# Attention in groups of two pairs, norms on GpSimd, half of the copies on VectorE

## The chip, the cores and the metric

The kernel runs on one core of a Trainium2 chip. The metric is the device time of one execution in microseconds. TensorE multiplies, VectorE (DVE) and ScalarE (ACT) work on its results in PSUM (8 banks) and on data in SBUF, GpSimd (POOL) on data in SBUF only, and SyncE starts the loads of the weights.

## What is computed

Two transformer blocks of two layers each on 512 tokens of width 1024, in fp32. The first block mixes NSA attention, a linear recurrence (RG-LRU) and a convolution with a layer norm. The second has attention layers (full A and windowed B with a sink in layer 0; latent C and neighbourhood D in layer 1), a cross attention X to a memory of 256 tokens, and a SwiGLU feed-forward. Cut to what the change touches, each attention is

```python
s = einsum('qd,kd->qk', q, k) * scale        # NSA, A, B, D: 64 wide; C: 64 + 32 (rope) wide
p = softmax(where(mask, s, NEG))             # NSA: times a gate per query and branch
o = einsum('qk,kd->qd', p, v)
```

with 8 heads of 64 and query blocks of 128. NSA has three branches (compressed keys, selected, window), whose gated outputs are added. The layer norm of the convolution is

```python
mu = mean(u); var = mean(square(u - mu))
un = (u - mu) * rsqrt(var + EPS) * ln_g + ln_b
```

## The kernel before, in words

The program is a list of stages (`PROGRAM`). Most of the span are matrix products: "strips" of 128 output columns, whose weights are loaded in pieces, split by ScalarE (high part, line 1226) and GpSimd (low part, line 2212, `w_lo`), and multiplied three times (lines 861 to 863). Between them stand seven attention stages: NSA twice, AB2, D2, C2, X2 twice.

An attention stage is a list of tiles: one head, 128 queries, up to 512 keys. Tiles come in pairs of two heads that use the two halves of TensorE's rows. NSA has 72 tiles (36 pairs), AB2 64, D2 and C2 32 each, X2 8. A tile goes through these steps, and every engine has its own program for them, which it runs in order:

- TensorE: `scores` (three products, lines 1067, 1070 and 1076; for compressed keys 1059) into one of 3 or 4 score banks.
- VectorE: `maxed` (lines 1933, 1935) scales, masks and takes the maximum; ScalarE: `exps` (1421) with the row sum.
- VectorE: `normed`: the reciprocal of a pair's two sums (1961), and two multiplications of a tile by its reciprocal, in NSA also by the gate (1965, 1967).
- TensorE: `turn` transposes the tile (1090) into bank 4 or 5; ScalarE: `copy` brings it back to SBUF (1432, ring `PT` of 4).
- TensorE: `values` (1100, 1103) into bank 6 or 7; VectorE: `output` (1977, 1979).

TensorE's order per pair s is: scores of pair s, turns of pair s - 2 (`TURN_LAG`), values of pair s - 3 (`VALUE_LAG`). VectorE and ScalarE go tile by tile. `extras(part)` hangs other work at numbered moments (one per tile): in NSA the layer norm of the convolution (sums and spreads over bank 0, `ln_sum`, `ln_spread`, `ln_var`, `ln_factor`, `ln_spread_factor`, lines 1153, 1159, 2012 to 2024; its squares on GpSimd in `layer_norm`, 2183 to 2193), high and low parts of the mixed output (`split`), and in D2 the load and scaling of biases. `DRAIN` gives the chunks of the next strip that TensorE does in the last steps of a stage, and `warm` (line 868) issues dummy products, in NSA in front of tile 30 too.

GpSimd runs through all pieces of weights in one loop; its layer norm and `rope_keys` stand at fixed pieces in it.

## Time and profile before

| | us |
|---|---|
| median of 3 runs | 2272.75 (2271.89 to 2274.1) |
| span of the profiled execution | 2275.0 |
| TensorE busy in it | 2199.9 (97%) |
| VectorE busy | 1246.9 (55%) |
| ScalarE busy | 1078.0 (47%) |
| GpSimd busy | 853.7 (38%) |

The profile is of one execution. Its own time is known as its span of 2275.0 us, from first to last instruction; it lies 2.25 us above the median. Busy time of TensorE is counted from modelled ends of pipelined products, so 97% doesn't mean full rate: what one instruction costs is the distance of its start to the next one's.

In the table by stage below (rows 2) the columns are: the stretch, its length in us, busy us (and instructions) of PE, PEld, DVE, ACT and POOL, the granted clock of TensorE as a share of 2.4 GHz, the DMA share and GB/s. A row of a timeline is: start and length in us, engine, line, operation, operands, how many, and in brackets the idle time before it and what ended it. The page's line of the chain (rows 1) gives shares of the span.

### The profile page before, as it was taken

The numbers are of one execution on the slowest core, as the hardware profiler recorded it, in microseconds if no ns is written. First come the engines' busy times: TensorE is split into PE (matmuls) and PEld (weight loads), VectorE is DVE, ScalarE is ACT, GpSimd is POOL, SyncE is SP. The second block draws the span as 40 slices with busy tenths as digits, with TensorE's granted clock in tenths as the row PEclk, the third lists the DMA queues.
The fourth block names the chain that finished last, engine by engine and source line by source line (L and its number), as shares of the span: only waits on it lengthen the run. The fifth ranks groups of instructions, "written<-read, shape, count | busy, mean of one in ns | idle before, by whom it ended". The sixth has DMA issues, their size and how long they took to land.

```text
span 2275.0 us, 33281 instructions
## 1 busy us (share of the span) xinstructions
PE 2199.9 (97%) x12130; PEld 1763.7 (78%) x12130; DVE 1246.9 (55%) x2614; ACT 1078.0 (47%) x2160; POOL 853.7 (38%) x665
## 2 busy tenths in 40 slices
PE   8999899999999999989999999999999999999997
PEld 6778667888866788668888888888767888888886
DVE  6997782499778446885552112234666655211222
ACT  6542484465247652685453223343566545322332
POOL 4333304443330343104255545554110425554553
PEclk9999899999999999999999999999999999999998
DMA  5334002332410233203233333343110323333331
GB/s 171 85 91 141 25 2 79 104 91 79 144 38 11 75 89 109 68 2 110 67 94 96 95 109 98 92 124 95 48 60 20 111 66 97 94 95 100 98 96 66
DMA packets 107186, 189.74 MB, mean 83 GB/s; under 512 B 12049, under 2 KB 22801, under 8 KB 106897
## 3 DMA queue, kind: packets, MB, share of 16 engines
q1 hardware_dynamic: 101136, 178.67, 27.3%
q10 hardware_dynamic: 5888, 8.95, 1.2%
q8 instruction: 99, 1.62, 0.3%
q14 instruction: 63, 0.51, 0.1%
HBM read 182.85 MB, written 2.10 MB: 81 GB/s over the span
## 4 chain that ended last, share of the span: by engine, by line
PE 85%; DVE 10%; issue 3%; ACT 2%; POOL 1%; DMA 0%; SPq 0%; DVEq 0%; ACTq 0%
PE bank L861 23%; PE bank L863 23%; PE bank L862 23%; PE bank L1090 3%; PE bank L1103 3%; PE bank L1076 2%; DVE temp L1933 1%; DVE bank L2053 1%; PE bank L868 1%; DVE temp L1965 1%; PE bank L1067 1%; PE bank L1070 1%; PE bank L931 1%; DVE temp L1967 1%; POOL w_lo L2212 1%
## 5 line engine op out<-in xcount | busy, mean ns | idle before, releaser
L2212 POOL TENSOR_TENSOR w_lo<-w_raw,w_hi 128x512 fp32r<-128x512 f32 (+3 forms) x618 | 824.7, 1341 | 1337.1 <-ACT w_hi L1226 1336.7
L861 PE MATMUL bank<-op_hi,w_hi 128*128 128x512 f32 x1840 | 734.4, 399 | 9.1 <-POOL w_lo L2212 4.4
L863 PE MATMUL bank<-op_hi,w_lo 128*128 128x512 f32 x1840 | 719.4, 391 | 0.0
L862 PE MATMUL bank<-op_lo,w_hi 128*128 128x512 f32 x1840 | 719.4, 391 | 0.0
L1226 ACT ACTIVATE w_hi<-w_raw 128x512 fp32r<-128x512 f32 (+2 forms) x634 | 385.4, 617 | 682.5 <-PE bank L863 678.8
L861 PEld LDWEIGHTS bank<-op_hi,w_hi 128*128 128x128 f32 x1840 | 347.1, 189 | 95.7 <-issue 15.3
L862 PEld LDWEIGHTS bank<-op_lo,w_hi 128*128 128x128 f32 x1840 | 347.6, 189 | 73.4 <-issue 4.1
L863 PEld LDWEIGHTS bank<-op_hi,w_lo 128*128 128x128 f32 x1840 | 347.1, 189 | 73.7
L1648 DVE TENSOR_TENSOR temp<-bank,rstd 128x512 f32<-128x512 f32 x151 | 104.4, 691 | 396.0 <-PE bank L863 378.2
L861 PE MATMUL bank<-side_hi,w_hi 128*128 128x512 f32 (+1 forms) x628 | 233.2, 371 | 2.5 <-DVE side_lo L1730 1.4
L863 PE MATMUL bank<-side_hi,w_lo 128*128 128x512 f32 (+1 forms) x628 | 230.9, 368 | 0.0
L862 PE MATMUL bank<-side_lo,w_hi 128*128 128x512 f32 (+1 forms) x628 | 230.8, 367 | 0.0
L1718 DVE TENSOR_TENSOR x_t<-bank,x_t 128x512 f32<-128x512 f32 x80 | 55.3, 691 | 314.3 <-PE bank L863 314.1
L1421 ACT ACTIVATE temp<-temp,small 128x512 f32<-128x512 f32 (+3 forms) x288 | 174.0, 604 | 14.0 <-DVE small L1933 6.7
L1432 ACT ACTIVATE temp<-bank 128x512 f32<-128x512 f32 (+3 forms) x304 | 140.8, 467 | 83.0 <-PE bank L1090 81.6
L2053 DVE SCALAR_TENSOR_TENSOR bank<-conv_area,par,bank 128x512 f32<-128x512 f32 x232 | 174.9, 754 | 6.8
L1090 PE MATMUL bank<-consts,temp 128*128 128x128 f32 x864 | 132.7, 283 | 34.2 <-DVE temp L1967 12.5
L1090 PEld LDWEIGHTS bank<-consts,temp 128*128 128x128 f32 x864 | 93.4, 141 | 81.6 <-issue 35.0
L861 PEld LDWEIGHTS bank<-side_hi,w_hi 128*128 128x128 f32 x628 | 118.4, 188 | 25.1 <-DVE side_lo L1730 2.7
L863 PEld LDWEIGHTS bank<-side_hi,w_lo 128*128 128x128 f32 x628 | 118.4, 188 | 19.6
L862 PEld LDWEIGHTS bank<-side_lo,w_hi 128*128 128x128 f32 x628 | 118.4, 189 | 19.4 <-issue 0.5
L1103 PE MATMUL bank<-temp,vz 128*64 128x128 f32 x1312 | 100.4, 290 | 0.0
(269 smaller groups left out, 2256.3 us busy)
## 6 DMA issues: line engine op xcount, KB each, us to landing
w_raw<-in_weights SPq DMA_DIRECT2D x620, 256.0 KB, 2.7
w_raw<-in_weights SPq DMA_DIRECT2D x32, 192.0 KB, 2.3
temp<-temp SPq DMA_DIRECT2D x40, 64.0 KB, 2.0
x_t<-in_x SPq DMA_DIRECT2D x8, 256.0 KB, 5.4
conv_area<-in_mem ACTq DMA_DIRECT2D x2, 1024.0 KB, 5.5
out_y<-ybuf SPq DMA_DIRECT2D x8, 256.0 KB, 2.1
conv_area<-in_bias ACTq DMA_DIRECT2D x1, 1920.0 KB, 8.0
conv_area<-in_bias ACTq DMA_DIRECT2D x2, 960.0 KB, 4.9
```

The costliest lines, as they stand in the source:

```text
L861: pe.matmul(dst, w[0], m[0], start=start, stop=False)
L862: pe.matmul(dst, w[0], m[1], start=False, stop=False)
L863: return pe.matmul(dst, w[1], m[0], start=False, stop=stop)
L1090: ins = pe.transpose(bank[4 + a % 2][:, P * b:P * b + P], E[a % E_RING][:, P * b:P * b + P], ident)
L1103: ins = pe.matmul(dst, t["pv"][b], PT[a % PT_RING][:, P * b:P * b + P], start=t["start"] and b == 0, stop=t["stop"] and last)
L1226: act.activation(w_hi[:, j, 0:m * w], w_raw[:, p % RAW_RING, 0:m * w], ACT.Copy).then_inc(*mark("weights_high", p))
L1421: act.activation(e, e, ACT.Exp, bias=m, scale=-1.0, accum_out=total).then_inc(*mark("exps", a))
L1432: act.activation(PT[a % PT_RING][:, 0:n], bank[4 + a % 2][:, 0:n], ACT.Copy).then_inc(*mark("probs_copied", a))
L1648: return dve.tensor_tensor(dst, strip_bank(n)[0:rows, 0:s.cols], f[0:rows, 0:s.cols], ALU.mult)
L1718: dve.tensor_tensor(x_t[:, s.idx, :], src[:, :], x_t[:, s.idx, :], ALU.add).then_inc(*mark("strip_taken", n))
L2053: settle(dve.scalar_tensor_tensor(out=acc[:, c, :] if j == CONV_K - 1 else run, in0=u_conv[:, c, j:j + T], scalar=w, in1=run, op0=ALU.mult ...
L2212: pool.tensor_tensor(w_lo[:, j, 0:n], w_raw[:, p % RAW_RING, 0:n], w_hi[:, j, 0:n].bitcast(F32), ALU.subtract).then_inc(*mark("weights_spl ...
```

## The change

Tiles of NSA, AB2, D2 and C2 are now worked on in groups of two pairs (`PAIRS`); X2 stays at one. TensorE's order per group s is: scores of both pairs of group s, values of group s - 2, turns of group s - 1. In C2 a group takes its two pairs from neighbouring head chunks, so that the four 32-wide rope parts lie in the four quarters of the rows; their products are issued for all four tiles behind both 64-wide parts. The norm multiplications of all tiles but NSA's compressed ones move from VectorE to GpSimd. Tiles 1 and 3 of a group are copied by VectorE instead of ScalarE. Groups write their outputs four tiles at a time (NSA: 18 as before, but with one output bank, 6). Score tiles use 4 banks throughout, turned tiles banks 4, 5 and a third; layer norm sums move to bank 7. The rings grow (`E_RING` 6 to 8), extras move to the end of a group's step, GpSimd's loop over pieces is cut by stages, with the layer norm spread over its steps.

```diff
-TURN_LAG = 2
-VALUE_LAG = 3
+PAIRS = {"NSA": 2, "AB2": 2, "D2": 2, "C2": 2, "X2": 1}
+TURN_LAG = {1: 2, 2: 1}
+VALUE_LAG = {1: 3, 2: 2}
+NEXT_SPLIT = 10
+VECTOR_COPIES = (1, 3)
-E_RING = 6
+E_RING = 8
-SCORES = (1, 2, 3)
+SCORES = (1, 2, 3, 0)
-WARM_TURN = {"NSA": {30: 3}, "AB2": {0: 1}, ...
+WARM_TURN = {"NSA": {}, "AB2": {0: 2}, ...
...
+                    t["out"], t["out_held"] = (6, at_group - 1) if step[1][0] == "NSA" else (6 + at_group % 2, at_group - 2)
+                    t["turn"] = 4 + n % 2
+                    if PAIRS[step[1][0]] == 2:
+                        third = t["out"] if step[1][0] != "NSA" else 7 if n >= LN_TILES else 4
+                        t["turn"] = (4, 5, third, 4 if third != 4 else 5)[n % 4]
...
+                def latent_scores(group):
...
+                    for pair in group:
+                        free_banks(pair)
+                        for x, y in parts:
+                            for t in pair:
+                                pe.matmul(score_bank(t), t["q"][x], t["k"][y], start=(x + y == 0), stop=False)
+                    for x, y in parts:
+                        for t in group[0] + group[1]:
+                            ins = pe.matmul(score_bank(t), t["more"][0][x], t["more"][1][y], start=False, stop=(x == 1))
...
+                    if PAIRS[part[0]] == 2:
+                        for pair in in_group(groups, s - value_lag):
+                            values(pair)
+                    for pair in in_group(groups, s - turn_lag):
+                        for t in pair:
+                            turn(t)
...
+                    if scaled_by_pool(part, t):
+                        dve.reciprocal(total, total).then_inc(*mark("sums_inverted", a))
+                        return
...
+                        for pair in before[:1]:
+                            normed(pair)
+                        for t in to_max[:2]:
+                            maxed(t)
+                        for pair in before[1:]:
+                            normed(pair)
+                        for t in to_max[2:3]:
+                            maxed(t)
+                        for t in [pair[1] for pair in in_group(groups, s - value_lag)]:
+                            if t["last"]:
+                                output(t)
+                        for t in to_copy[:1]:
+                            copy(t)
+                        for t in to_max[3:]:
+                            maxed(t)
+                        for t in to_copy[1:]:
+                            copy(t)
...
+            def attend(part):
+                groups, l = groups_of(part), part[1]
+                def scaled(pair):
+                    t = pair[0]
+                    pool.wait_ge(*after("sums_inverted", pair[1]["a"]))
+                    total, _ = pair_sums(t)
+                    for r, t in enumerate(pair):
+                        e = E[t["a"] % E_RING][:, 0:t["nk"]]
+                        if t["gate"] is not None:
+                            ins = pool.tensor_scalar(e, e, total[:, r:r + 1], t["gate"], ALU.mult, ALU.mult)
+                        else:
+                            ins = pool.tensor_scalar(e, e, total[:, r:r + 1], C("ones")[:, 0:1], ALU.mult, ALU.mult)
+                        ins.then_inc(*mark("probs_scaled", t["a"]))
+                if part[0] == "NSA":
+                    norm_added(l)
+                for s in range(steps_of(part)):
+                    if part[0] == "NSA" and s == 7:
+                        norm_squares(l, 0, 2)
+                    for pair in in_group(groups, s - 1):
+                        if scaled_by_pool(part, pair[0]):
+                            scaled(pair)
+                    if NEXT_SPLIT in moments_of(part, s):
+                        split_to(last_of(FOLLOWS[part] + 1))
...
```

## Rows read from the trace of the kernel before

**Rows 1.** The page: share of the span of each engine on the chain.

```profile
PE 85%; DVE 10%; issue 3%; ACT 2%; POOL 1%; DMA 0%; SPq 0%; DVEq 0%; ACTq 0%
```

**Rows 2.** Busy time by stage: NSA, AB2, D2, C2; columns below.

```profile
241.70:352.50 110.80, 100.44 (x903) 72.51 (x903) 85.48 (x294) 78.55 (x227) 13.76 (x12) 0.92 0.03 6
...
927.80:1024.80 97.00, 87.88 (x844) 63.95 (x844) 82.89 (x311) 82.25 (x236) 5.36 (x4) 1.00 0.08 23
1617.60:1673.00 55.40, 51.75 (x495) 37.64 (x495) 43.76 (x131) 43.05 (x102) 2.59 (x4) 1.00 0.13 40
1694.40:1763.70 69.30, 69.30 (x606) 48.16 (x606) 45.14 (x134) 45.64 (x107) 5.38 (x4) 1.00 0.11 32
```

**Rows 3.** Timeline of TensorE, one pair of AB2: start, length, line, count.

```profile
951.95 0.50 PE L1076 MATMUL bank<-side_hi 64*128 64x512 f32 x2
...
952.86 1.09 PE L1090 MATMUL bank<-consts,temp 128*128 128x128 f32 x8
953.88 1.09 PE L1103 MATMUL bank<-temp,vz 128*64 128x128 f32 x16
954.91 0.50 PE L1076 MATMUL bank<-side_hi 64*128 64x512 f32 x2
```

**Rows 4.** Timeline of TensorE, AB2's windowed tiles, four pairs.

```profile
998.67 0.45 PE L1076 MATMUL bank<-side_hi 64*128 64x384 f32 x2
...
1009.26 0.44 PE L1076 MATMUL bank<-side_hi 64*128 64x384 f32 x2
...
1010.98 0.67 PE L1090 MATMUL bank<-consts,temp 128*128 128x128 f32 x4 [0.92 <-DVE temp L1967]
```

**Rows 5.** Timeline of TensorE, start of AB2, two pairs of scores.

```profile
928.39 0.39 PE L1076 MATMUL bank<-side_hi,side_lo 64*128 64x512 f32 x2
928.62 0.40 PE L1076 MATMUL bank<-side_hi 64*128 64x512 f32 x2
```

**Rows 6.** Short stretches of transposes and values; line 1090 (min/median/max ns).

```profile
950.40 0.60 PE L1090 MATMUL bank<-consts,temp 128*128 128x128 f32 x4
...
951.42 0.61 PE L1103 MATMUL bank<-temp,vz 128*64 128x128 f32 x8
...
L1090 PE MATMUL bank<-consts,temp x864: 270/273/473, 251.8 to 1873.3; 128*128 128x128 f32 x173
```

**Rows 7.** Timeline of TensorE, one pair of C2.

```profile
1714.14 0.50 PE L1067 MATMUL bank<-op_hi 64*128 64x512 f32 x2
...
1715.04 0.50 PE L1070 MATMUL bank<-side_hi 32*128 32x512 f32 x2
...
1715.93 1.11 PE L1090 MATMUL bank<-consts,temp 128*128 128x128 f32 x8
...
1717.99 0.50 PE L1067 MATMUL bank<-op_hi 64*128 64x512 f32 x2
```

**Rows 8.** Instructions by form, VectorE, AB2: count | busy us, mean ns.

```profile
L1935 DVE TENSOR_SCALAR_CACHE_REDUCE temp<-bank 128x512 f32<-128x512 f32 x32 | 21.5, 685 | 4.8 <-PE bank L1076 4.8
L1967 DVE TENSOR_SCALAR temp<-temp,small 128x512 f32<-128x512 f32 x32 | 16.0, 541 | 0.6
...
L1961 DVE RECIPROCAL small<-small 128x2 f32<-128x2 f32 x32 | 5.2, 163 | 0.6
```

**Rows 9.** Instructions by form, GpSimd, whole span.

```profile
L2212 POOL TENSOR_TENSOR w_lo<-w_raw,w_hi 128x512 fp32r<-128x512 f32 x572 | 783.8, 1377 | 1219.1 <-ACT w_hi L1226 1218.6
...
L2190 POOL TENSOR_TENSOR conv_area<-conv_area 128x512 f32<-128x512 f32 x8 | 8.3, 1040 | 42.9 <-DVE conv_area L2012 42.9
...
L2202 POOL CAST side_hi<-temp 128x512 fp32r<-128x512 f32 x1 | 0.6, 612 | 0.0
```

**Rows 10.** Timeline of VectorE while GpSimd splits weights.

```profile
945.71 1.53 DVE L1967 TENSOR_SCALAR temp<-temp,small 128x512 f32<-128x512 f32 x2
```

**Rows 11.** Timeline of TensorE, NSA, in front of the second spread.

```profile
291.93 2.84 PE L868 MATMUL bank<-consts 128*128 128x512 f32 x6
295.25 1.00 PE L1090 MATMUL bank<-consts,temp 128*128 128x128 f32 x6 [0.48 <-DVE temp L1965]
```

More of the change, by code:

```diff
@@ L278, in build @@
         sp8 = sb("sp8", [P, 8])
[L279 removed]
+        small = sb("small", [P, 256])
         PAD = CONV_K - 1
@@ L600, in build @@
                     t["a"], t["g"] = at_tile, at_group
-                    banks = SCORES if step[1][0] == "NSA" and at_tile - ts[0]["a"] < LN_TILES else SCORES + (0,)
-                    t["bank"] = banks[(at_tile - ts[0]["a"]) % len(banks)]
+                    n = at_tile - ts[0]["a"]
+                    t["bank"] = SCORES[n % len(SCORES)]
                     t["held"] = held.get(t["bank"])
@@ L765, in score_bank, with grouped, by_vector, copied @@
             return bank[t["bank"]][:, 0:t["nk"]]
+        def grouped(part):
+            return PAIRS[part[0]] == 2
+        def by_vector(part, t):
+            return grouped(part) and (t["a"] - ATT[part][0]["a"]) % 4 in VECTOR_COPIES
+        def copied(part, a):
+            t = ATT[part][a - ATT[part][0]["a"]]
+            return after("probs_copied_vector" if by_vector(part, t) else "probs_copied", a)
+        def scaled_by_pool(part, t):
+            return grouped(part) and not t["cmp"]
         def tables_of(s):
@@ L1039, in attend, with free_banks, scores @@
                 steps = DRAIN[part[0]]
-                def scores(pair):
-                    for t in pair:
+                def free_banks(tiles_of):
+                    for t in tiles_of:
                         if t["held"] is not None:
                             pe.wait_ge(*after("maxed", t["held"]))
-                        if part[0] == "NSA" and t["a"] == ts[LN_TILES]["a"]:
-                            pe.wait_ge(*after("ln_scaled", (part[1], 3)))
-                    if part[0] == "C2" and pair is pairs[0]:
+                def latent_scores(group):
+                    parts = ((0, 0), (0, 1), (1, 0))
+                    if group[0][0]["a"] == ts[0]["a"]:
                         pe.wait_ge(*after("rope_keys", 0))
+                    for pair in group:
[6 more added lines that the diff above has]
+                            ins = pe.matmul(score_bank(t), t["more"][0][x], t["more"][1][y], start=False, stop=(x == 1))
+                            if x == 1:
+                                ins.then_inc(*mark("scores", t["a"]))
+                def scores(pair):
+                    free_banks(pair)
                     if pair[0]["cmp"]:
@@ L1108, in values @@
                     for t in pair:
-                        pe.wait_ge(*after("probs_copied", t["a"]))
-                        if t["first"] and t["g"] >= 2:
-                            pe.wait_ge(*after("outputs_taken", t["g"] - 2))
+                        pe.wait_ge(*copied(part, t["a"]))
+                        if t["first"] and t["out_held"] >= 0:
+                            pe.wait_ge(*after("outputs_taken", t["out_held"]))
+                        if t["first"] and t["size"] == 4:
+                            pe.wait_ge(*copied(part, t["a"] + 2))
                     blocks = range(len(pair[0]["pv"]))
@@ L1984, in attend @@
+                for s in range(steps_of(part)):
+                    if NEXT_SPLIT in moments_of(part, s):
                         split_to(last_of(FOLLOWS[part] + 1))
-                    if i < len(ts):
-                        maxed(ts[i])
-                    if NORM_LAG <= i < len(ts) + NORM_LAG and i % 2 == 1:
-                        normed(ts[i - NORM_LAG:i - NORM_LAG + 2])
-                    if OUT_LAG <= i < len(ts) + OUT_LAG and ts[i - OUT_LAG]["last"]:
-                        output(ts[i - OUT_LAG])
@@ L1991, in attend @@
[L1991 to L1996 removed]
+                    now, before = in_group(groups, s), in_group(groups, s - 1)
+                    if PAIRS[part[0]] == 1:
+                        for t in [t for pair in now for t in pair][:1]:
+                            maxed(t)
+                        for t in [pair[1] for pair in in_group(groups, s - value_lag - 1)]:
+                            if t["last"]:
+                                output(t)
+                        for t in [t for pair in now for t in pair][1:]:
+                            maxed(t)
+                        for pair in before:
+                            normed(pair)
+                    else:
+                        to_max = [t for pair in now for t in pair]
+                        to_copy = [t for pair in before for t in pair if by_vector(part, t)]
+                        for pair in before[:1]:
[3 more added lines that the diff above has]
+                        for pair in before[1:]:
+                            normed(pair)
+                        for t in to_max[2:3]:
+                            maxed(t)
+                        for t in [pair[1] for pair in in_group(groups, s - value_lag)]:
+                            if t["last"]:
+                                output(t)
+                        for t in to_copy[:1]:
+                            copy(t)
+                        for t in to_max[3:]:
+                            maxed(t)
+                        for t in to_copy[1:]:
+                            copy(t)
@@ L1998, in extra_stage @@
+                    for i in moments_of(part, s):
+                        for stage in between.get(i - LOW_LAG[PAIRS[part[0]]], ()):
+                            if stage[0] in LATE_LOWS:
+                                extra_stage(*stage)
+                        for stage in between.get(i, ()):
+                            if stage[0] not in LATE_LOWS:
+                                extra_stage(*stage)
             def extra_stage(kind, l, c=None):
```

275 lines of the change are left out of this document (158 added, 117 removed).

## The prediction

> **What bounds the kernel now.** I read the chain of work that ended last first: TensorE carries 85% of it, GpSimd 1% [rows 1]. So what counts is TensorE's own work plus its waits. The change touches only the attention stages. The second view is the table of busy time by stage [rows 2]: the two NSA stages (one row is shown, 110.8 us; the other lasts 112.6 us and looks the same), AB2 97.0, D2 55.4 and C2 69.3 us, 445 us in all. The reader is to see three things there. TensorE is idle for 10.4, 9.1, 3.6 and 0.0 us in the four kinds. VectorE and ScalarE are at 71 to 85% in NSA and AB2, GpSimd at 5 to 12% everywhere. And the granted clock is 0.92 in NSA and 1.00 elsewhere.
>
> The third view is TensorE's timeline in the first half of AB2 (full rows of 512 keys) [rows 3]. One pair takes 2.96 us (951.95 to 954.91) with no idle: scores 0.91, eight transposes 1.02, sixteen value instructions 1.03. So here TensorE is the bound, and no relief of the other engines helps by itself. The second half of AB2 differs: four pairs take 10.59 us (998.67 to 1009.26), 2.65 each, and TensorE stands 0.92 us for VectorE's scaled tile [rows 4]. There VectorE is the bound.
>
> **What the regrouping takes off TensorE.** Inside a pair TensorE changes three times between ways of using its array: half-height (scores), full (transposes), half-width (values). What a change costs is read by comparing with runs without one. At the start of AB2 two pairs of scores stand directly behind each other: the last pass of one begins at 928.39, the first pass of the next at 928.62, 0.23 us [rows 5]. Three such passes are 0.69 us; the pair above takes 0.91. Four transposes without a change among them last 0.60, of which the last one's own length is 0.273 (the median of that line): 0.11 us each, 0.87 for eight, against 1.02 [rows 6]. Value instructions run two by two: eight last 0.61, 0.11 us per two, 0.87 for sixteen, against 1.03 [rows 6]. Sum without changes 2.43, with them 2.96: I take 0.50 us per pair for all three. The changed kernel does scores of two pairs, values of two, turns of two: the same three changes per two pairs. That saves 0.25 us a pair wherever TensorE is the bound.
>
> **C2 gains more.** Its scores have a part of 64 rows (1714.14 to 1715.04, 0.90 us) and a part of 32 rows (to 1715.93, 0.89 us), and one pair takes 3.85 us [rows 7]. The change does both 64-row parts, then one 32-row part in which the four tiles of a group sit in four different quarters of the array. Per group, before: 2 x 1.79 = 3.58. After: 0.91 + 3 x 0.23 = 1.60, plus 0.89 if four small products run side by side as two do now: 2.49. Saved 1.09, plus 0.30 from the two other kinds of change: 1.39 per group, 8 groups, 11.1 us. Bounds for the four side by side: 0.69 us more per group (5.5 us in all) if they run two by two, nothing if all four overlap. I take nothing, since two of 32 rows take as long as two of 64 [rows 7]: the rows in use don't set the time. The Trainium skill ("TensorE: Matmul & The Clock Gate", section Measured speedup vs the span model) gives 3.07 times, not 4, for four tiles of 32 rows; by it, as an estimate, the block would be a third longer and C2 would gain 1.7 us less. No row here shows four at once.
>
> **What GpSimd gets, and whether it is covered.** VectorE's two norm multiplications (541 ns each [rows 8]) leave it, and two copies of turned tiles per group come to it from ScalarE. The same copy from PSUM has no row on VectorE; a 512-wide op from PSUM takes 685 ns there [rows 8]. Per group of full tiles VectorE then has 4 x 0.69 of maxima, 2 x 0.16 of reciprocals, 2 x 0.69 of copies and one output: under 4.9 us against 5.9 now on TensorE. It isn't the bound. GpSimd's multiplication of a 128x512 tile by two scalars has no row. From below: its one-input cast of that size takes 612 ns. From above: its two-input subtraction takes 1377 ns [rows 9]. The new op reads one tensor as the cast does, so I take 0.7 us, and keep 0.61 to 1.38. The Trainium skill ("GPSIMD Engine Reference", Elementwise side-by-side cycle accounting) names 769 ns for a well unrolled loop over 512 elements; at that price the sum below doesn't change. Its section Engine selection says to keep elementwise work off this engine, which speaks against this change and is rival 3.
>
> The four multiplications of a group are serial, and their place in the chain decides. VectorE's order is: ..., copy of tile 1, maximum of tile 3, copy of tile 3, then the first reciprocal of that next group. The copy of tile 3 waits for TensorE's last transposes of the step. So the loop is: transposes of tile 3 (0.60), copy (0.69), reciprocal (0.16 [rows 8]), four multiplications, transposes of tile 3 again, with some 0.2 us of hand-offs (estimate): 1.65 + 4p. Where p is 0.7 that is 4.5 us, hidden behind TensorE's 2 x 2.71 = 5.4. With the copy of tile 1 and the last maximum in front of it the chain allows p up to about 0.87; from p = 1.06 the loop is longer than the 5.9 us of today. GpSimd does no harm to VectorE's reads of PSUM: the maxima take 685 ns on average. It does to VectorE's doubled-rate multiplications: two of them took 1.53 us at 945.7 [rows 10], while GpSimd was splitting weights, against a mean of 541 ns for one [rows 8]. These leave VectorE, so this stops.
>
> **The sum by stage**, against the profiled execution of 2275.0 us:
> AB2, full tiles: 16 pairs x 0.25 = 4.0 us.
> AB2, windowed tiles: VectorE loses two multiplications a pair and gets one copy; TensorE's floor falls too. I take 0.25 a pair here as well, 4.0 us. Bounds 0 (the in-order waits for turned tiles eat it) and 10 (TensorE's floor).
> D2: 16 x 0.25 = 4.0, and 0.5 from VectorE's freed time beside the bias scaling: 4.5.
> C2: 11.1.
> NSA, each: 36 x 0.25 = 9.0. Against it: the single output bank, where values of a new head pair wait within a step for VectorE's output (twice, about 1.4 each: 2.8); the square root of the layer norm, whose spread now stands in the same step as its factor. TensorE bridges this with 2.84 us of dummy products (removed by the change) and stands 0.48 more [rows 11], 3.3 us; after the change ScalarE comes to the root only behind its last exponential of the step, and I expect a bare wait of 4.5, 1.2 more. At the end all four silu stages come in one step and the first value of the next strip comes later: 1.2. Fewer waits for VectorE and ScalarE in the narrow tiles: +1.2 back (bounds 0 and 7, the larger part of the idle time). Net 5.0 each, 10.0 for both.
> Weight splits: in AB2 and C2 four pieces are now queued on GpSimd in front of a group's multiplications, 4 x 1.377 = 5.5 us [rows 9]. The slack of that step covers about 3 of it: 2.5 and 2.0 lost. In NSA the seven layer norm ops (1040 ns and more [rows 9]) stand between multiplications too, but tiles are narrow there: covered, and 8 us on the path per stage if p is high.
> Sum: 4.0 + 4.0 + 4.5 + 11.1 + 10.0 - 4.5 = 29.1 us. The profiled execution would take 2245.9 us; it lies 2.25 us above the median of 2272.75, so the median goes to 2243.6. I say 2244.
>
> **Rivals.**
> 1. The forecast, 2244: p below 0.9, changes of array use halved. Speaks for it: rows 3 to 7 price the changes directly. Chance 0.55.
> 2. NSA also gets its clock back and loses its idle time. A mean clock of 0.92 over 110.8 us is 8.9 us per stage, 17 in all: 2272.75 - 29 - 17 = 2227. For: fewer idle gaps. Against: the table-load wait stays. Chance 0.12.
> 3. GpSimd is the bound, at p = 1.3. Loop 1.65 + 5.2 = 6.85 against 5.9: +0.95 in 16 groups of AB2 and D2, +15. C2 about -2 (its step is 7.7 now). NSA: +0.5 in 18 groups and 6 for the layer norm, +15 each, +30. Weight splits uncovered in AB2, D2 and C2: +2. Total +45: 2318. It decides from p = 1.06. For: all its two-input ops of this size take 1.04 to 1.38. Against: the cast at 612 ns. Chance 0.17.
> 4. The change doesn't do what it says: the PE waits take the place of the array changes, because turned tiles, copies and maxima stand in one order on VectorE, and p is near 1. Then only C2's packing (9) and a few us remain: 2262. It speaks for it that the lag from scores to turns is now one step, and the sum of all waits in one step counts. Chance 0.16.
>
> **How the numbers follow.** Two times within 0.2% (4.5 us) can't be told apart for this kernel. Faster: rivals 1 and 2 whole and most of 4, 0.55 + 0.12 + 0.10 = 0.77. Same: 0.05, the slow end of rival 4. Slower: 0.17 + 0.01 = 0.18. Range 2218 to 2290: it takes in the unknown C2 packing, both ends of AB2's windowed half, rival 4, rival 2 and the mild part of rival 3 (p to 1.15), and leaves out the rest of 3 and what lies beyond 2.
>
> **What the profile after would show.** In AB2's first half a group period of 5.4 us with scores x4, values x32, transposes x16 and no idle in front of the transposes: right; 6 or more with transposes waiting for GpSimd: rival 3. GpSimd's 128x512 row by two scalars: 0.6 to 0.9 right, over 1.06 wrong. In C2 a 32-row block of 0.9 us for four tiles and a group of 6.3 us; a block of 1.6 would take 5.5 us away. In NSA idle time in front of the first value of a new head pair and one of about 4.5 us in front of the second spread; a clock of 1.0 there speaks for rival 2. Outside the attention stages nothing should move by more than 1 us; if it does, the ordering of weight splits on GpSimd is what I missed.

## The result

The changed kernel takes 2294.8 us (median, 2287.46 to 2296.41), against 2273.43 for the kernel before in the same comparison. The ratio is 1.0077, 95% interval 1.0057 to 1.0096: slower by 0.77%, 17.5 us (the two medians lie 21.4 apart). The forecast was 2244, range 2218 to 2290, so the time lies outside the range, on the wrong side: the time was to fall and it rose. Timed again beside the kernel before, the changed one gives 1.0073 (1.0054 to 1.0092).

Where the time went is read best as distances from the start of one attention stage to the start of the next (the first score product of each). These rows are the table of busy time for the changed kernel, from NSA 1 to NSA 2, NSA 2 to AB2, AB2 to the first X2, D2 to C2, and C2 to the second X2. Columns are those of rows 2.

```profile
241.80:666.60 424.80, 398.45 (x2246) 321.35 (x2246) 281.60 (x567) 199.66 (x385) 178.81 (x173) 0.95 0.25 73
666.60:956.00 289.40, 265.42 (x1690) 212.19 (x1690) 165.69 (x418) 132.88 (x302) 119.91 (x126) 0.93 0.22 62
956.00:1139.80 183.80, 175.12 (x1337) 141.56 (x1337) 121.68 (x346) 114.02 (x286) 88.91 (x96) 1.00 0.22 64
1642.30:1717.80 75.50, 67.49 (x567) 49.75 (x566) 53.75 (x132) 46.07 (x111) 34.67 (x48) 1.00 0.19 59
1717.80:1872.00 154.20, 150.07 (x1098) 122.31 (x1097) 87.07 (x194) 82.32 (x173) 70.21 (x64) 0.99 0.27 76
```

The same distances in the kernel before, its second NSA stage as a row, the others in the table behind it:

```profile
650.80:927.80 277.00, 263.97 (x1696) 204.72 (x1696) 176.25 (x446) 143.99 (x338) 82.27 (x62) 0.97 0.23 65
```

| from | before | after | measured | forecast |
|---|---|---|---|---|
| NSA 1 | 409.1 | 424.8 | +15.7 | -5.0 |
| NSA 2 | 277.0 | 289.4 | +12.4 | -5.0 |
| AB2 | 187.3 | 183.8 | -3.5 | -5.5 |
| D2 | 76.9 | 75.5 | -1.4 | -4.5 |
| C2 | 159.6 | 154.2 | -5.4 | -9.1 |
| sum | | | +17.8 | -29.1 |

The spans differ by 2292.9 - 2275.0 = 17.9 us, so nothing else moved. AB2, D2 and C2 went the forecast way, by 10.3 instead of 19.1 us. The two NSA stages turned the sign. The NSA windows themselves answer to the first line of rows 2:

```profile
241.80:368.30 126.50, 103.89 (x897) 81.45 (x897) 75.09 (x266) 67.46 (x191) 51.84 (x76) 0.82 0.02 6
666.60:791.50 124.90, 102.33 (x897) 80.08 (x897) 75.04 (x266) 67.44 (x191) 51.77 (x76) 0.84 0.02 6
```

TensorE is idle for 22.6 us instead of 10.4, and its granted clock is 0.82 instead of 0.92. VectorE and ScalarE have less to do than before (75 and 67 us against 85 and 79), so no engine became the bound. The second view is TensorE's list of waits, longest sums first:

```profile
PE bank L911 <- DVE op_lo L1667: 12.1, 2, 6.0
PE bank L1228 <- DVE small L2151: 8.2, 2, 4.1
PE bank L1149 <- POOL temp L2343: 7.9, 6, 2.2
```

Two of them, once per NSA stage each, are new: 6.0 us in front of the next strip (it needs the silus), and 4.1 us in front of the second spread. In rows 11 the place of the second had 2.84 us of dummy products and 0.48 us of wait. What the clock did behind the 4.1 us is seen in a narrow window of each kernel, ten microseconds from where TensorE goes on; the changed kernel stands first, then the kernel before at the same place of its program:

```profile
299.50:309.50 10.00, 10.00 (x73) 9.00 (x71) 2.21 (x8) 1.44 (x2) 2.71 (x4) 0.50 0.01 2
```

```profile
295.00:305.00 10.00, 9.17 (x106) 7.65 (x106) 8.05 (x28) 5.97 (x17) 0.00 (x0) 1.00 0.01 2
```

0.50 is the 1.2 GHz level. TensorE is busy for all of those 10.00 us and gets 73 instructions started; the kernel before starts 106 in 9.17 busy us at 2.4 GHz. (The mix of products is not quite the same, so the counts show the direction and not the exact price.)

A third stretch of half clock comes earlier in the stage, in the changed kernel:

```profile
275.50:289.10 13.60, 12.10 (x76) 8.93 (x76) 5.94 (x27) 5.61 (x20) 7.38 (x11) 0.50 0.01 2
```

No wait of TensorE around its start is longer than 1.47 us. In the second NSA stage it lasts as long (from 698.8); the kernel before has 6.8 us of half clock at this place in its first stage and 3.4 in its second.

In the distance of NSA 2 the parts can be told apart. Idle time went from 277.00 - 263.97 = 13.0 to 289.40 - 265.42 = 24.0 us: +11.0. A granted clock of c over t us costs (1 - c) x t while TensorE is busy: 0.03 x 277.0 = 8.3 before, 0.07 x 289.4 = 20.3 after, +12.0 (each to about 1.4, since the clock is given in hundredths). Together +23, of which +12.4 were seen. So TensorE's own work at full clock became some 10.5 us shorter; 2.84 of it are the dummy products, and the rest fits the array changes, which no run tested in NSA by themselves. The forecast for the same three terms was +6.8 of idle time (2.8 + 4.0 + 1.2 - 1.2), nothing for the clock, and -11.8 of work (9.0 and the 2.84 of dummy products). So the forecast of the work was near; idle time was 4 us short, and the clock was missing.

### The profile page after: what moved, and what is told of

Same layout as the page of the kernel before. It is cut to its first block, busy times and chain, and to the rows that moved or that the text cites. A ratio compares the mean times of both kernels' runs of the same rounds, so it can differ in the third digit from the quotient of the medians.

```text
span 2292.9 us, 33268 instructions
## 1 busy us (share of the span) xinstructions
PE 2192.0 (96%) x12120; PEld 1780.0 (78%) x12120; DVE 1205.9 (53%) x2462; ACT 1027.1 (45%) x2024; POOL 1021.7 (45%) x921
## 3 DMA queue, kind: packets, MB, share of 16 engines
q8 instruction: 99, 1.62, 0.3%
## 4 chain that ended last, share of the span: by engine, by line
PE 86%; DVE 7%; issue 2%; ACT 2%; POOL 2%; DMA 0%; SPq 0%; DVEq 0%; ACTq 0%
PE bank L911 23%; PE bank L913 23%; PE bank L912 23%; PE bank L1149 4%; PE bank L1162 4%; PE bank L1129 3%; DVE bank L2183 1%; POOL w_lo L2384 1%; PE bank L918 1%; DVE temp L2024 1%; PE bank L981 1%; PE bank L1123 1%; PE bank L1030 1%; PE bank L1108 0%; POOL temp L2345 0%
## 5 line engine op out<-in xcount | busy, mean ns | idle before, releaser
L911 PE MATMUL bank<-op_hi,w_hi 128*128 128x512 f32 x1840 | 733.4, 399 | 20.3 <-DVE op_lo L1667 12.1
L2345 POOL TENSOR_SCALAR temp<-temp,small,consts 128x512 f32<-128x512 f32 (+2 forms) x128 | 92.2, 733 | 118.4 <-DVE small L2053 118.3
L2343 POOL TENSOR_SCALAR temp<-temp,small,gates 128x128 f32<-128x128 f32 (+3 forms) x128 | 76.8, 612 | 121.6 <-DVE small L2053 121.6
```

The source lines that it names most:

```text
L911: pe.matmul(dst, w[0], m[0], start=start, stop=False)
L2343: ins = pool.tensor_scalar(e, e, total[:, r:r + 1], t["gate"], ALU.mult, ALU.mult)
L2345: ins = pool.tensor_scalar(e, e, total[:, r:r + 1], C("ones")[:, 0:1], ALU.mult, ALU.mult)
```

## Experiments

Theory A: the NSA stages lose by two new waits and, more than that, by the half clock that follows a standstill (a time in which TensorE does nothing). Rivals: the waits alone are the loss (B), or GpSimd's multiplications are (C).

### Both waits removed

```diff
-DRAIN = {"NSA": ((), (0, 0), (), (0, 0, 1, 1, 1, 1)),
+DRAIN = {"NSA": ((), (), (), (0, 1, 0, 1, 0, 1, 0, 1)),
-    at(37 + c, "ln_scale", l, c)
-    at(72 + c // 2, "ln_silu", l, c)
-    at(74 + c // 2, "ln_split", l, c)
+    at(40 + c, "ln_scale", l, c)
+    at(72 + c, "ln_silu", l, c)
+    at(72 + c, "ln_split", l, c)
-at(72, "gate_silu", l)
+at(76, "gate_silu", l)
-at(35, "ln_spread_factor", l)
+at(38, "ln_spread_factor", l)
```

> Two edits of the changed kernel's NSA stage at once: the second spread of the layer norm stands one step later (moment 38, its scalings at 40 to 43), and at the end each silu is followed at once by its own high part, the gate's silu comes last, and TensorE does the last values before it starts the next strip. Theory A (bare waits in NSA cost their own time and pull the clock down): an NSA stage up to the next strip goes from 126.5 us to about 108, the whole from 2295 to 2258, below the kernel before (2273). Theory B (the clock falls because of the grouping of narrow tiles, whatever the waits): only the waits of 4.1 and 6.0 us go, 116 us per stage, the whole about 2275, granted clock in NSA stays near 0.82.

Measured: 2264.01 us, ratio to the kernel before 0.9958 (0.9937 to 0.9979). Table of busy time, the NSA windows of this kernel:

```profile
243.30:348.40 105.10, 90.02 (x890) 70.00 (x890) 72.42 (x262) 62.56 (x184) 51.73 (x76) 0.94 0.02 6
651.30:756.40 105.10, 89.74 (x890) 69.34 (x890) 72.28 (x262) 62.88 (x183) 51.84 (x76) 0.94 0.02 7
```

The two orders cost the changed kernel its loss: 27 us came back by the two ratios (31 by the medians), and the result is faster than both kernels. It lies between A's 2258 and B's 2275, nearer to A, and the clock in the windows is 0.94, not B's 0.82. GpSimd's busy time is as in the changed kernel (51.7 against 51.8), which speaks against C. The end of the stage was reordered, so the windows don't hold the same products (890 against 897); the distances do. The two NSA distances together fell from 714.2 to 682.3 us. Of these 31.9 us, 8.7 are idle time (50.3 to 41.6) and 23.2 busy time with the same work: the clock is the larger part.

### Each wait alone

The spread alone is the lines with `ln_scale` and `ln_spread_factor` of the diff above; the end alone is the rest of it.

> Only the second spread and its scalings moved one step later. Both theories: the wait of 4.11 us in front of it goes. Theory A: the 10.2 us at half clock behind it go too, 5 us more, NSA 126.5 to 117. Theory B: the clock falls all the same, NSA 122.5.

> Only the end of NSA: silu and high part in turn, gate silu last, last values before the next strip. Theory A: the wait of 6.03 us shrinks to 1 or 2, the half clock behind it (6.8 us) goes; last values and two rows of the next strip are done 7 us earlier, NSA 126.5 to about 119. Rival: the table load and the four silus set the time of the next strip in any order, gain under 3 us.

Measured, one execution each: 2273.19 and 2285.58 us. The two NSA distances sum to 694.0 us with the spread mended, 703.7 with the end mended and 682.3 with both. In the changed kernel they sum to 714.2, but to 706.5 in its second profile (the run further down), because there the first stage's stretch of half clock at 275 lasts 3.4 us instead of 13.7. So single executions can't price the waits closely: the spread is worth 12 to 20 us for the two stages, the end 3 to 12. The second NSA stage gives a like comparison for the spread, since that stretch lasts 13.7 us in both profiles of the changed kernel and in this one. Its distance with the spread mended:

```profile
653.40:936.10 282.70, 260.34 (x1692) 207.13 (x1692) 164.80 (x418) 132.98 (x302) 120.25 (x126) 0.95 0.22 63
```

Against 289.40 with 265.42 busy, 6.7 us are gone, 5.1 of them busy time and only 1.6 idle time, since other waits grew. So the wait of 4.1 us cost some 6.7 us here, and most of that was clock.

### The norms back on VectorE

```diff
 def scaled_by_pool(part, t):
-    return grouped(part) and not t["cmp"]
+    return False
```

(VectorE's `normed` multiplies by sum and gate instead.)

> The norm multiplications of the grouped stages go back to VectorE, all else as in the changed kernel. Theory A: GpSimd is not what costs in NSA, which stays within 3 us of 126.5; in AB2 VectorE has 6.0 us of work per group of full tiles against TensorE's 5.4, so AB2 gets 4 to 6 us longer than 92.8. Rival C (the hand-over to GpSimd is the loss, since TensorE waits 1.05 and 2.17 us for it in narrow groups): NSA gets 5 us or more shorter.

Measured: 2339.78 us, one execution. C falls: the distances of the two NSA stages grew by 10.8 and 13.7 us where C wanted them shorter, and within this grouping the multiplications on GpSimd are worth 45 us. The expectation was off too, since it had NSA within 3 us and AB2 4 to 6 longer; AB2's distance grew by 11.7. A full group of AB2 takes 5.94 us instead of 5.42, so VectorE doesn't carry them beside two copies per group. The granted clock of the whole execution is 0.968, against 0.977 in the changed kernel: more waits, less clock again.

### Dummy products in the waits

If the half clock behind a standstill is the loss, filling the wait with products that nobody needs should bring time back, though nothing that counts moves.

```diff
 elif kind in ("ln_spread", "ln_spread_factor"):
+    if kind == "ln_spread_factor":
+        pe.wait_ge(*after("ln_mean_square", l))
+        warm(7, 3)
     pe.wait_ge(*after("ln_mean" if kind == "ln_spread" else "ln_factor", l))
```

> The changed kernel with one addition: in front of the second spread of each NSA stage TensorE runs three dummy products of 512 columns (2.8 us, as the kernel before had them) as soon as VectorE has read the variance sums, inside the 4.1 us in which it stood still at 299.04. Nothing that anyone waits for moves: VectorE's factor is still ready at 298.98, so the spread starts at the same moment. Theory A (half of the loss in NSA is the granted clock, which falls behind such a standstill): the half-clock stretch at 299.5 (10.2 us) goes or shrinks to one of 3.4, and each NSA stage is 3 to 6 us shorter; the run comes out 6 to 12 us below the changed kernel, 2283 to 2289 us. Theory B (the waits alone cost the time, and the clock falls for its own reasons): no change, 2292 to 2297 us.

Measured: 2280.19 us, ratio 1.0012 (0.9997 to 1.0027). That is 14.6 us below the changed kernel's 2294.8 and 10.9 below the 2291.13 of its second timing; by the ratios some 14. A expected 6 to 12. Timeline of TensorE at the spread, and the ten microseconds behind it:

```profile
296.37 2.84 PE L918 MATMUL bank<-consts 128*128 128x512 f32 x6 [0.72 <-DVE small L2148]
299.76 1.16 PE L1231 MATMUL bank<-consts,small 128*128 128x128 f32 x8 [0.54 <-DVE small L2154]
```

```profile
299.80:309.80 10.00, 9.75 (x103) 8.57 (x105) 3.98 (x13) 3.33 (x7) 3.03 (x4) 0.83 0.01 2
```

The spread still starts where VectorE's factor lets it, 0.72 + 2.84 + 0.54 = 4.10 us behind the work in front. Behind it the clock is 0.83 instead of 0.50, and 103 instructions start instead of 73. B falls: the 4.1 us weren't shortened, only filled.

The counterpart is the kernel before without its dummy products:

```diff
-WARM_TURN = {"NSA": {30: 3}, "AB2": {0: 1}, "D2": {0: 2}, "C2": {0: 2}, "X2": {0: 2}}
+WARM_TURN = {"NSA": {}, "AB2": {0: 1}, "D2": {0: 2}, "C2": {0: 2}, "X2": {0: 2}}
```

> The kernel before, with one thing taken away: the three dummy products of 2.84 us that fill the wait at 291.93 in each NSA stage (those that the change also removes). No one waits for them, so by the waits alone nothing moves: TensorE stands still for 3.3 us and goes on at 295.25 as it does now. Theory A (the clock falls behind a standstill, and that is a large part of the loss): a half-clock stretch of some 7 to 10 us appears behind 295, each NSA stage is 3 to 5 us longer, the run 6 to 10 us above the kernel before. Theory B: no difference, within 2 us of the kernel before.

Measured: 2278.52 us, ratio 1.0013 (1.0003 to 1.0022): 3 us, between A's 6 to 10 and B's 2 at most, so by its time this run doesn't decide. Timeline at the wait, then the windows behind it:

```profile
295.85 1.51 PE L1090 MATMUL bank<-consts,temp 128*128 128x128 f32 x6 [3.33 <-DVE temp L1965]
```

```profile
295.90:299.10 3.20, 3.20 (x19) 2.54 (x20) 2.49 (x8) 2.33 (x7) 0.00 (x0) 0.50 0.02 5
299.30:309.30 10.00, 9.20 (x112) 7.61 (x110) 7.44 (x28) 4.66 (x15) 0.00 (x0) 1.00 0.00 1
```

The clock fell here too, but was back after 3.4 us, where the changed kernel stayed at half clock for 10.2. So a standstill of 3.33 us and one of 4.11 are not priced alike. In the changed kernel the 13.7 us of half clock had ended 5.7 us before the wait; between them TensorE was nearly always busy (0.3 us idle from 288.00 to the wait). Whether the length, what went before or what came behind makes the difference wasn't settled.

Two more runs put dummy products at the stage's end as well, and the first missed its place.

```diff
+if part[0] == "NSA":
+    warm(3, 11)
 drain(part, steps[3])
```

> The changed kernel once more, on the same chip as the next run, so that the two can be set side by side. If the fall of the granted clock in the NSA stages is a property of the kernel, 2290 to 2297 us again and some 40 us of half clock per NSA stage; if it is partly chance, single executions scatter between 2280 and 2297 with half-clock stretches between 27 and 48 us per stage.

> The changed kernel with dummy products in two of its waits in each NSA stage: three in front of the second spread (the run before with these alone gave 2280) and eleven of 512 columns (about 4.9 us) behind the last transposes, inside the 6.03 us in which TensorE waits at 362.25 for the silus. No product that counts is moved. Theory A (what follows a standstill is half clock, and that is most of the loss): the half-clock stretch of 6.8 us at 360.8 and its twin at 784.1 go, another 3 us each, 2272 to 2277, 18 to 22 us below the changed kernel of this call with all its waits still there. Theory B (the waits themselves are the loss): no difference between this run and the changed kernel beyond 3 us.

Measured: the changed kernel again 2291.13 (2287.05 to 2297.49); the one with dummy products 2298.79. The half clock is partly chance: in this profile of the same kernel the first NSA stage's distance is 417.3 us instead of 424.8, the second's 289.2 (289.4). The stretch behind the spread is in both stages 10.2 us long again, but in the first it began 2.5 us before the wait's end. The 6.03 us are in front of the second drain of strips, not the last, and eleven products are 22 instructions:

```profile
361.80 9.71 PE L918 MATMUL bank<-consts 128*128 128x512 f32 x22
```

The next product that counts starts at 370.94, so 9.1 us a stage are added work. Without them 2298.8 - 18.2 = 2280.6: 10.5 us below the changed kernel beside it, and in line with the run that has the spread's dummy products alone. The second form has six products where the wait is:

```diff
+if part[0] == "NSA" and s - len(groups) == 1:
+    warm(3, 6)
 if 0 <= s - len(groups) < 3:
     drain(part, steps[s - len(groups)])
```

> The changed kernel with three dummy products in front of the second spread of each NSA stage (as e5) and six (12 instructions, 5.3 us) directly behind the transposes that end at 356.2, in the 6.03 us in which TensorE waits for the silus. Nothing that counts is moved. Theory A (half clock follows a standstill): the half-clock stretch of 6.8 us behind it goes in both stages, 3 us each, the run 5 to 7 us below e5's 2280, 2273 to 2275. Theory B: no difference from e5, 2279 to 2281.

Measured: 2276.62 us, ratio 0.9999 (0.9988 to 1.001). The clock behind the wait, in the changed kernel (behind 6.03 us of standstill) and here (behind 0.89):

```profile
361.00:367.60 6.60, 5.35 (x30) 4.36 (x32) 2.50 (x4) 1.94 (x4) 0.00 (x0) 0.50 0.01 2
```

```profile
357.50:364.10 6.60, 5.84 (x48) 4.75 (x49) 3.96 (x7) 2.61 (x5) 0.28 (x1) 1.00 0.01 2
```

Here the stretch of half clock is gone, as A says. In the total it brings 3.6 us against the spread's dummies alone (A expected 5 to 7), and the two intervals overlap, so this share is shown in the windows and only likely in the time. With both, the changed kernel stands level with the kernel before: its whole loss, 0.77%, was bought back with products that compute nothing, which B can't explain. Removing the waits themselves brings another 0.4%.

### Array use, C2's packing, GpSimd's loop

The first puts scores, values and turns of AB2 and D2 back pair by pair inside a group.

```diff
+if part[0] in ("AB2", "D2"):
+    for k in range(2):
+        if k:
+            for pair in in_group(groups, s)[1:]:
+                scores(pair)
+        for pair in in_group(groups, s - value_lag)[k:k + 1]:
+            values(pair)
+        for pair in in_group(groups, s - turn_lag)[k:k + 1]:
+            for t in pair:
+                turn(t)
```

> The changed kernel, but within a group of AB2 and D2 scores, values and transposes are done pair by pair, so that TensorE changes its way of using the array six times per group instead of three. By the forecast a set of three changes costs 0.50 us: the period of a full group goes from 5.42 back to 5.9, AB2 about 4 us longer (8 full groups by 0.5) and D2 some 3. If the gain of the full groups did not come from these changes but from VectorE's freed time, the period stays at 5.42.

Measured: 2327.42 us, one execution. The period of a full group is 6.7, not 5.9; AB2's distance grew by 19.0 us and D2's by 11.8, where 4 and 3 were expected. Timeline of TensorE, score and transpose rows of one group:

```profile
977.95 0.50 PE L1129 MATMUL bank<-side_hi 64*128 64x512 f32 x2
...
979.87 1.09 PE L1149 MATMUL bank<-consts,temp 128*128 128x128 f32 x8
980.89 0.50 PE L1129 MATMUL bank<-side_hi 64*128 64x512 f32 x2
...
983.33 1.38 PE L1149 MATMUL bank<-consts,temp 128*128 128x128 f32 x8 [0.45 <-POOL temp L2355]
984.64 0.50 PE L1129 MATMUL bank<-side_hi 64*128 64x512 f32 x2
```

The half that doesn't wait lasts 980.89 - 977.95 = 2.94 us, as long as a pair of the kernel before (rows 3: 2.96). Two such halves are 5.88 against 5.42, the period in the changed kernel:

```profile
982.88 0.50 PE L1129 MATMUL bank<-side_hi 64*128 64x512 f32 x2
988.30 0.50 PE L1129 MATMUL bank<-side_hi 64*128 64x512 f32 x2
```

So three changes cost 0.46, and a pair saves 0.23 (forecast 0.25). The other half takes 3.75: TensorE stands 0.45 us for GpSimd's products in front of the transposes, which then take 1.31 instead of 1.02. The expectation hadn't that. It reads as if grouping didn't only save changes, but also gave the chain of maximum, exponential and multiplication the time to run; no run tests this by itself.

The second takes C2's 32-row parts pair by pair.

```diff
-for x, y in parts:
-    for t in group[0] + group[1]:
+for pair in group:
+    for x, y in parts:
+        for t in pair:
```

> The changed kernel, but C2's 32-row score parts are done for two tiles at a time instead of four. If four small products ran side by side as fast as two (the forecast), the part grows from 0.9 to 1.6 us: +0.69 us per group, C2's windows 5.5 us longer. If the hardware already ran them two by two, nothing changes. By a quarter lost of the fourfold overlap, +0.4 per group.

Measured: 2285.08 us, one execution; C2's distance 152.9 against 154.2, and its group still 6.33. Timeline of TensorE, the 32-row part, in the changed kernel and then in this one:

```profile
1746.04 0.51 PE L1111 MATMUL bank<-side_hi 32*128 32x512 f32 x4
1746.37 0.40 PE L1111 MATMUL bank<-side_lo,side_hi 32*128 32x512 f32 x4
1746.61 0.40 PE L1111 MATMUL bank<-side_hi,side_lo 32*128 32x512 f32 x4
```

```profile
1743.35 0.52 PE L1112 MATMUL bank<-side_hi 32*128 32x512 f32 x4
1743.69 0.42 PE L1112 MATMUL bank<-side_lo,side_hi 32*128 32x512 f32 x4
1743.92 0.42 PE L1112 MATMUL bank<-side_hi,side_lo 32*128 32x512 f32 x4
```

Twelve products of 32 rows take 0.9 us in either order; the second pair's first products start beside the first pair's, although four others stand ahead of them in the program. So the edit didn't make two by two out of four at once, and can't price that; what it shows is that four products on the four quarters take no longer than the two of rows 7 did, whatever the order. The forecast's 0.89 for the block holds. The Trainium skill ("TensorE: Matmul & The Clock Gate", Measured speedup vs the span model) gives 3.07 times for four tiles of 32 rows, by which the block would be longer; this trace doesn't show that, with 0.90 us for twelve.

The third doubles GpSimd's price of a tile.

```diff
+if part[0] in ("AB2", "D2"):
+    ins.then_inc(*mark("pool_step"))
+    pool.wait_ge(*after("pool_step"))
+    ins = pool.tensor_scalar(e, e, C("ones")[:, 0:1], C("ones")[:, 0:1], ALU.mult, ALU.mult)
 ins.then_inc(*mark("probs_scaled", t["a"]))
```

> The changed kernel, but GpSimd multiplies each tile of AB2 and D2 a second time, by ones: p goes from 0.77 to 1.6 us. By the loop that I wrote down (1.65 + 4p, TensorE's floor 5.42) the period of a full group becomes 8.0 us: +2.6 in each of some 7 full groups of AB2 and 8 of D2, narrow groups +1.5: D2 +18, AB2 +30. If GpSimd's product is hidden with much more slack than the loop says (the loop is wrong), the period stays near 5.4 to 6.5.

Measured: 2363.84 us, one execution. Timeline of GpSimd, the first multiplication of two groups:

```profile
988.64 0.77 POOL L2345 TENSOR_SCALAR temp<-temp,small,consts 128x512 f32<-128x512 f32 x1 [2.13 <-DVE small L2053]
...
990.26 0.77 POOL L2345 TENSOR_SCALAR temp<-temp,small,consts 128x512 f32<-128x512 f32 x1
...
996.82 0.77 POOL L2345 TENSOR_SCALAR temp<-temp,small,consts 128x512 f32<-128x512 f32 x1 [1.67 <-DVE small L2053]
```

A tile now costs 990.26 - 988.64 = 1.62 us, the period is 996.82 - 988.64 = 8.18. The loop that the prediction wrote down gives 1.65 + 4 x 1.62 = 8.13. AB2's distance rose by 43 us (183.8 to 227.1), D2's by 26.5, more than the expected 30 and 18: their clocks fell to 0.91 and 0.88, which comes to some 20 and 12 us.

### Weight pieces one per step

```diff
 if NEXT_SPLIT in moments_of(part, s):
-    split_to(last_of(FOLLOWS[part] + 1))
+    split_to(STRIPS[FOLLOWS[part]].pieces[0] if part[0] in ("AB2", "C2") else last_of(FOLLOWS[part] + 1))
+for i in range(3):
+    if part[0] in ("AB2", "C2") and NEXT_SPLIT + 4 * i + 4 in moments_of(part, s):
+        split_to(STRIPS[FOLLOWS[part]].pieces[0] + i + 1)
```

> The kernel with both NSA orders mended (spread and tail), and in AB2 and C2 the four pieces of the next weight strip are split one per step (moments 10, 14, 18, 22) instead of all four at moment 10. If the AB2 group of 7.13 us and the C2 group of 8.11 us are long because four subtractions of 1.38 us stand in front of GpSimd's multiplications, each falls by 1.7 us (to 5.42 and 6.32) and the run comes out 3 us below the mended kernel, 2260 to 2262 us. If the pieces only move the same wait into four groups, nothing changes: 2264.

Measured: 2262.59 us, ratio 0.994 (0.992 to 0.996), the lowest median here; against the run with both waits removed (0.9958) the intervals overlap, so the gain stands in the rows and not in the time. AB2's distance is 181.6 (183.8), C2's 152.6 (154.2). AB2's group of 7.13 us fell to 5.42: the slack of a group swallows one piece of 1.38 us, not four.

With two more dummy products where NSA waits for 1.04 and 1.47 us:

```diff
-WARM_TURN = {"NSA": {}, "AB2": {0: 2}, "D2": {0: 2}, "C2": {0: 2}, "X2": {0: 2}}
+WARM_TURN = {"NSA": {20: 2}, "AB2": {0: 2}, "D2": {0: 2}, "C2": {0: 2}, "X2": {0: 2}}
```

> The kernel with both NSA orders mended and the pieces spread out, and two dummy products of 512 columns (0.9 us at full clock) in front of tile 20's transposes in each NSA stage, where TensorE stands for 1.04 and then 1.47 us. Theory A: a half-clock stretch of 3.4 us per stage goes, 1 to 2 us per stage less, 2259 to 2261. Theory B: nothing, or up to 0.9 us more per stage where the dummies outlast the wait: 2262 to 2265.

Measured: 2264.32 us, ratio 0.9943 (0.9925 to 0.9961): no gain. The ten microseconds behind these waits, in this kernel's first NSA stage:

```profile
276.00:286.00 10.00, 8.11 (x48) 5.88 (x49) 3.41 (x16) 1.59 (x6) 5.17 (x8) 0.50 0.00 0
```

The clock is at half all the same, so 0.9 us of dummy products doesn't hold it. What makes it fall at this place, where small tiles and waits of 1.0 and 1.5 us come together, stayed open. It is the third stretch of the result: 13.7 us long in three of the four NSA stages of the changed kernel's two profiles, 3.4 in the other, and still 13.7 us in one stage of the kernel with both waits removed. So theory A covers the clock behind the two large waits, and not this part.

## Why the prediction was wrong

**The step that failed is the term for NSA.** It said -5.0 us a stage and came out as +15.7 and +12.4. The working counted idle time and never what the granted clock does behind it, a term put at nothing without a reason. The clock stood in the prediction only as something to be won (rival 2, 2227 us), and rows 2 already showed it at 0.92 in NSA, so it could go down as well as up. The change took away the dummy products that bridged one wait, and I priced that as "a bare wait of 4.5, 1.2 more". The wait was 4.1, near the 4.5 expected; mending it was worth 6 to 10 us a stage, 6.7 in the like comparison. Of the 46.9 us between the forecast and the profiled execution, the clock in the two NSA stages makes some 24, their idle time 10, their work 4 (a little less was saved than forecast), and AB2, D2 and C2 together 9. A stretch of half clock costs half of TensorE's busy time in it; by that, both stages together pay some 10 us behind the spread, 5 at the end, and in the third stretch 7 more than the kernel before. The cause is shown for the two large waits; for the third stretch it stays open.

**The second mis-sized term is the end of the stage**, 1.2 us. Timeline of TensorE and of ScalarE in the changed kernel:

```profile
362.25 0.77 PE L911 MATMUL bank<-op_hi,w_hi 128*128 128x512 f32 x1 [6.03 <-DVE op_lo L1667]
```

```profile
355.51 0.60 ACT L1501 ACTIVATE temp<-bank 128x512 f32<-128x512 f32 x1 [0.91 <-PE bank L1149]
356.12 1.28 ACT L1550 ACT_TABLE_LOAD   x1
357.42 1.52 ACT L1550 ACTIVATE conv_area<-conv_area,par 128x512 f32<-128x512 f32 x2
358.84 0.61 ACT L1356 ACTIVATE ybuf<-ybuf 128x512 f32<-128x512 f32 x1
359.36 1.50 ACT L1550 ACTIVATE conv_area<-conv_area,par 128x512 f32<-128x512 f32 x2
360.77 2.18 ACT L1299 ACTIVATE op_hi<-conv_area 128x512 fp32r<-128x512 f32 x4
```

The last copy, a table load, four silus with a gate's silu among them, then the first high part, behind which VectorE starts its low parts at 361.41: one chain from 355.51 to 362.25. The strip stands first in TensorE's order, the last values behind it. The prediction saw that the silus come together, but counted only their delay and not that a strip was queued in front of them. Mending it gave 1.4 to 5.9 us a stage, by which profiles are compared.

**AB2**: the group period is 5.42 as forecast (5.90 for two pairs before). The windowed half gave 0.20 a pair instead of 0.25 (four pairs 9.80 us against the 10.59 of rows 4), the weight pieces cost 2.2 (forecast 2.5), and the first and last group of a stage don't save what a steady one does: -3.5 instead of -5.5. **D2**: the plain groups are at 5.42. The groups with bias scaling take 7.40:

```profile
1663.06 2.34 DVE L1918 SCALAR_TENSOR_TENSOR conv_area<-conv_area 128x960 f32<-128x960 f32 x2
1665.43 0.17 DVE L2053 RECIPROCAL small<-small 128x2 f32<-128x2 f32 x1
```

```profile
1666.61 2.90 PE L1149 MATMUL bank<-consts,temp 128*128 128x128 f32 x16 [1.00 <-POOL temp L2345]
```

VectorE (first fence) scales the bias for 2.34 us and comes to its reciprocal at 1665.43; GpSimd's products stand behind that, and TensorE (second fence) waits for them. I had these groups as a gain. **C2**: a group takes 6.32, where the sum said 7.70 - 1.39 = 6.31. Two of them take 8.11 and 7.97; with the pieces spread out the second falls to 6.32, and of the first 1.3 us are likely half clock, since it is 6.81 in the run with C2's parts pair by pair, where C2's clock stays at 1.00.

**Right** were the price of a multiplication on GpSimd (page of line groups by form, in the changed kernel), the loop (8.18 us measured against its 8.13, at a tile of 1.62 us; its break-even at 1.06 was not tried), and that rival 3 wouldn't come:

```profile
L2345 POOL TENSOR_SCALAR temp<-temp,small,consts 128x512 f32<-128x512 f32 x96 | 73.0, 774 | 98.4 <-DVE small L2053 98.3
L2343 POOL TENSOR_SCALAR temp<-temp,small,gates 128x384 f32<-128x384 f32 x32 | 20.9, 665 | 21.5 <-DVE small L2053 21.5
L2343 POOL TENSOR_SCALAR temp<-temp,small,gates 128x256 f32<-128x256 f32 x32 | 17.5, 558 | 20.5 <-DVE small L2053 20.5
L2343 POOL TENSOR_SCALAR temp<-temp,small,gates 128x128 f32<-128x128 f32 x32 | 14.1, 452 | 43.6 <-DVE small L2053 43.5
```

774 ns against the 0.7 us that I took; the 769 ns of the Trainium skill ("GPSIMD Engine Reference", Elementwise side-by-side cycle accounting) fits better. The Trainium skill's advice, in Engine selection of the same page, to keep elementwise work off GpSimd didn't decide here: within this grouping, moving it back costs 45 us. The wait for the output bank was 0.87 us against 1.4.

The range failed for the same reason as the sum. Its slow end came from rival 3 alone; no case had waits that grow and a clock that falls with them. That the time came within 5 us of the range's end says nothing for the working.

## What to carry to other kernels

Price a wait of TensorE with what follows it, not only with its length: here 4.1 us of standstill cost about 7, and dummy products in it brought some 5 to 7 a stage back. If a change removes dummy products or gathers several small waits into one, treat the granted clock as a term with its own sign, above all in a stage that is already below 1.00. And when work is regrouped, write down for each in-order engine what now stands directly in front of each cross-engine product; both waits here went away by moving entries of two lists.

## What the runs showed of the hardware

- The clock was at 1.2 GHz for 10.2 us behind a standstill of 4.11 us (in one of four cases it fell inside the wait); behind one of 3.33 us for 3.4. Around one of 6.03 us it was so for 6.8 us, 1.4 of them still in the wait. With no wait over 1.5 us beside it, it was at 1.2 GHz for 13.7 us.
- Executions of the changed kernel ran from 2287.05 to 2297.49 us with mean clocks from 0.981 down to 0.976, in step: the half clock is partly chance, and so is the time.
- Products on different quarters of the array pass each other: a later pair's start at 1743.37, 0.02 us behind an earlier pair's, ahead of four others (at 1743.69 and 1743.92) that stand in front of them in the program.
- GpSimd's multiplication by two scalars takes 452, 558, 665 and 774 ns for 128, 256, 384 and 512 elements: some 345 ns and 0.84 ns per element.
